# Scale, shift and the first input rows by quarters of the features, with rotary swaps as VectorE shuffles

## The reference, cut to what matters

```python
    cos, sin = _rope_tables(positions)
    c_act = jax.nn.silu(c)
    mod = (c_act @ w_ada[l] + b_ada[l])[:, None, :]
    shift1, scale1, gate1, shift2, scale2, gate2 = jnp.split(mod, N_MOD, axis=-1)
    h = _rmsnorm(x, g_mix[l]) * (1.0 + scale1) + shift1
    proj = h @ w_in[l]
    a_u, a_v, b_q, b_k, b_v, c_q, c_k, c_v = jnp.split(proj, splits, axis=-1)
    ...
    y_c = _dilated_window(_rope(c_q...), _rope(c_k...), c_v...)
    # _rope: x1, x2 = jnp.split(x, 2, axis=-1)   (halves of each head of 64)
    #        concatenate([x1 * cos - x2 * sin, x2 * cos + x1 * sin])
```

## Time and profile before

| | before |
|---|---|
| median of 3 runs | 935.67 us |
| profiled execution | 936.85 us |
| its span, first to last instruction | 935.0 us |
| PE busy | 907.0 us (97%) |
| DVE busy | 613.3 us (66%) |
| ACT busy | 497.1 us (53%) |

### The profile page before, as it was taken

The page is one execution under the profiler, slowest core; times in us unless marked ns, Lnnn a source line. Parts: engine busy times, 40 slices in busy tenths (PEclk is TensorE's granted clock), DMA queues, the critical chain, the costliest instruction groups (busy, mean ns, idle before and its releaser), DMA issues.

```text
span 935.0 us, 17321 instructions
## 1 busy us (share of the span) xinstructions
PE 907.0 (97%) x7189; PEld 839.9 (90%) x7189; DVE 613.3 (66%) x958; ACT 497.1 (53%) x729; POOL 0.2 (0%) x4
## 2 busy tenths in 40 slices
PE   5899999999999999999999999999999999999997
PEld 2688788899999999778999999998999999988886
DVE  0565685786776776787765555576886765566664
ACT  4537674754555567665644343346656653344333
POOL 0000000000000000000000000000000000000000
PEclk9899999999999999999999999999999999999999
DMA  9988757675556569415366565555442655555541
GB/s 351 369 292 275 271 182 249 211 254 204 171 175 218 180 169 179 105 46 163 109 216 195 195 195 196 179 181 180 128 143 95 222 176 172 188 186 181 181 135 45
DMA packets 130697, 176.78 MB, mean 189 GB/s; under 512 B 19696, under 2 KB 108188, under 8 KB 130620
## 3 DMA queue, kind: packets, MB, share of 16 engines
q1 hardware_dynamic: 129852, 173.51, 57.0%
q10 hardware_dynamic: 768, 2.16, 0.7%
HBM read 174.62 MB, written 1.05 MB: 188 GB/s over the span
## 4 chain that ended last, share of the span: by engine, by line
PE 84%; DVE 7%; ACT 4%; DMA 3%; issue 2%; SPq 0%; ACTq 0%; DVEq 0%
PE psum L1605 25%; PE psum L1597 21%; PE psum L1598 21%; PE psum L1601 4%; PE psum L1602 4%; DMA raw<-in_w_ada_dram 2%; DVE w_lo L956 2%; PE psum L1699 1%; ACT w_hi L526 1%; PE psum L2199 1%; PE psum L2154 1%; PE psum L2143 1%; PE psum L2133 1%; DMA raw<-in_w_in_dram 1%; DVE h_lo L994 1%
## 5 line engine op out<-in xcount | busy, mean ns | idle before, releaser
L526 ACT ACTIVATE w_hi<-raw 128x2048 fp32r<-128x2048 f32 (+1 forms) x139 | 264.5, 1905 | 147.4 <-PE psum L1605 122.1
L1597 PE MATMUL psum<-h_hi,w_hi 128*128 128x256 f32 x1352 | 328.7, 283 | 1.5 <-DVE h_lo L1128 1.1
L956 DVE TENSOR_TENSOR w_lo<-raw,w_hi 128x2048 fp32r<-128x2048 f32 (+1 forms) x139 | 313.2, 2278 | 22.2 <-ACT w_hi L526 22.1
L1598 PE MATMUL psum<-h_lo,w_hi 128*128 128x256 f32 x1352 | 324.5, 279 | 0.0
L1597 PEld LDWEIGHTS psum<-h_hi,w_hi 128*128 128x128 f32 x1352 | 254.4, 188 | 10.2 <-issue 7.2
L1598 PEld LDWEIGHTS psum<-h_lo,w_hi 128*128 128x128 f32 x1352 | 254.8, 188 | 0.8
L1605 PE MATMUL psum<-h_hi,w_lo 128*128 128x256 f32 x1352 | 186.9, 280 | 0.7 <-DVE w_lo L956 0.5
L1605 PEld LDWEIGHTS psum<-h_hi,w_lo 128*128 128x128 f32 x1352 | 170.3, 188 | 1.5 <-DVE w_lo L956 1.4
L1324 DVE SCALAR_TENSOR_TENSOR arena<-psum,rstd 128x256 f32<-128x256 f32 x64 | 26.9, 424 | 131.9 <-PE psum L1605 130.0
L1597 PE MATMUL psum<-a_hi,w_hi 128*128 128x256 f32 x464 | 110.6, 280 | 0.6 <-DVE a_lo L1311 0.4
L1598 PE MATMUL psum<-a_lo,w_hi 128*128 128x256 f32 x464 | 110.2, 279 | 0.0
(11 more groups left out here) (272 smaller groups left out, 899.3 us busy)
## 6 DMA issues: line engine op xcount, KB each, us to landing
raw<-in_mlp_w_in_dram SPq DMA_DIRECT2D x32, 1024.0 KB, 5.6
raw<-in_mlp_w_out_dram SPq DMA_DIRECT2D x32, 1024.0 KB, 7.1
raw<-in_w_ada_dram SPq DMA_DIRECT2D x24, 1024.0 KB, 7.6
raw<-in_w_up_dram SPq DMA_DIRECT2D x22, 1024.0 KB, 5.1
raw<-in_gla_w_in_dram SPq DMA_DIRECT2D x12, 1024.0 KB, 5.3
raw<-in_w_down_dram SPq DMA_DIRECT2D x11, 1024.0 KB, 5.4
raw<-in_w_in_dram SPq DMA_DIRECT2D x10, 1024.0 KB, 7.5
raw<-in_w_out_dram SPq DMA_DIRECT2D x4, 1024.0 KB, 5.9
```

The costliest lines, as they stand in the source:

```text
L526: act.activation(halved(w_hi, m % SPLIT_SLOTS, SPLITS[m]), halved(raw, r % RAW_SLOTS, SPLITS[m]), ACT.Copy).then_inc(*mark("w_hi", m))
L956: dve.tensor_tensor(halved(w_lo, m % SPLIT_SLOTS, key), halved(raw, r % RAW_SLOTS, key), halved(w_hi, m % SPLIT_SLOTS, key).bitcast(F32), ...
L1597: pe.matmul(dst, high, both[0], start=start, stop=False, skip_group_check=True)
L1598: return pe.matmul(dst, high, both[1], start=False, stop=False, skip_group_check=True)
```

## The change

- The condition chunks of scale and shift now hold 256 columns of all 1024 rows, so that one chunk gives a finished quarter of scale or of shift (`part`). `w_in` is loaded for the first four projection chunks (1024 output features) by 256 rows, that is by quarters of the input features (`rows_in`). The stream starts with four times scale quarter, shift quarter, input rows: 12 MB.
- Eight sums (four chunks of two tiles) are kept in banks 0 to 3 and grow from quarter to quarter (`rows_high`, `rows_low`); they are read in `evict`. The ring is banks 4 to 6 meanwhile.
- `turn_x` comes ahead of all condition chunks, and DVE copies half of x.
- Rotary: `w_hi` and `w_lo` of queries and keys are written with their columns in bands of 16, so that the swap is one within 32 lanes. DVE does it with a shuffle, five instructions of 128 x 512 or 128 x 256 for two tiles, and PE does nothing. The rounding of such rows is three instructions in place of one, on ACT and on DVE.
- Of the other condition chunks four come beside `in` 0 to 3 no more but beside the output projection.

```diff
-ADA_BESIDE = [0, 1, 1, 2, 1, 1, 1, 1, 2, 1, 1]
+ADA_BESIDE = {4: 1, 5: 1, 6: 1, 7: 1, 8: 1, 9: 1, 10: 2}
+ADA_BESIDE_OUT = [2, 1, 1, 0]
+FIRST_CHUNKS = 4
...
+    for q in range(4):
+        s += [("ada", 1, q), ("ada", 0, q), ("rows_in", q)]
...
+    s = [("setup",), ("turn_x",), ("root", 0), ("part", 1, 0), ("part", 0, 0), ("quarters", 0), ("rows", 1), ("mod", 1, 0),
+         ("mod", 0, 0), ("gains", 0, 0), ("total", 0), ("normed", 0, 0), ("round", 0), ("first", 0), ("round_low", 0)]
+    for q in range(1, 4):
+        s += [("rows_high", q - 1, 0), ("part", 1, q), ("rows_high", q - 1, 1), ("part", 0, q), ("mod", 1, q), ("gains", 0, q),
+              ("normed", 0, q), ("rows_low", q - 1, 0), ("mod", 0, q), ("rows_low", q - 1, 1), ("round", q), ("first", q),
+              ("sines",) if q == 2 else ("angles",) if q == 1 else ("round", 4), ("round_low", q)]
+    s += [("rows_high", 3, 0), ("rows_high", 3, 1), ("rows_low", 3, 0), ("rows_low", 3, 1),
+          ("evict", 0), ("rope", 0), ("evict", 1), ("round_low", 4), ("evict", 2), ("evict", 3)]
+    extra = {4: [("rope", 1), ("rope", 2), ("w_sp",)],
+             5: [("win_a", 0), ("win_a", 1), ("rows", 2), ("rows", 3), ("rows", 4), ("win_a", 2)],
...
+                    if SPLITS[m][0] == "rows_in":
+                        for h in range(2):
+                            act.activation(banded(w_hi, m % SPLIT_SLOTS)[:, :, :, h, :],
+                                           banded_raw(r % RAW_SLOTS)[:, :, :, h, :], ACT.Copy).then_inc(*mark("w_hi_banded", m, h))
+                        act.activation(w_hi[:, m % SPLIT_SLOTS, QK:CHUNK], raw[:, r % RAW_SLOTS, QK:CHUNK], ACT.Copy)\
+                            .then_inc(*mark("w_hi", m))
...
+            def part(p, q):
...
+                for j in range(2):
+                    for g in range(4):
+                        ins = pe.matmul(dst[32 * g:32 * g + 32, 0:S], c_rep[:, 4 * j + g, :], src[:, 4 * j + g, :], start=(j == 0),
+                                        stop=(j == 1), skip_group_check=True)
...
+            def rows_high(q, j):
...
+                for n in range(FIRST_CHUNKS):
...
+                    for m in range(2):
+                        high_by_both(first_sum(n, m), row_tile(w_hi, slot, j, n, m), (h_hi[:, k, :], h_lo[:, k, :]),
+                                     k == 0 and m == 0)
...
+                dve.wait_ge(*at("act_read", "in", n, 1))
...
+                dve.stream_shuffle(work[:, 2:4, :], both, SWAPPED).then_inc(*mark("rope_swapped", n))
+                dve.tensor_tensor(work[:, 0:2, :], both, angle_of(1), ALU.mult).then_inc(*mark("rope_cos", n))
...
+                dve.tensor_tensor(work[:, 2:4, :], work[:, 2:4, :], angle_of(0), ALU.mult).then_inc(*mark("rope_sin", n))
...
+                for m in range(2):
...
+                    dve.tensor_tensor(dst, work[:, m, :], work[:, 2 + m, :], ALU.add).then_inc(*mark("roped", n, m))
```

307 lines of the change are left out of this document (156 added, 151 removed).

## The result

The changed kernel takes 951.87 us (median of four runs, 950.28 to 956.91), against 935.71 us for the kernel before, run beside it (four runs, 935.48 to 935.76). The ratio is 1.0166, with a 95% interval of 1.0139 to 1.0193. It is slower, as forecast, but by twice the size: 16.2 us where 7.8 was forecast (943.5, with a range that ended at 948).

What follows compares the result with a forecast made beforehand. PE, busy 97%, was taken as the bound. Eight sums end at T = 60.2 (57.0 plus 3.2 for the clock); T - 52.33 gives +7.9 on 936.85, 944.7 profiled, median 943.5; eight in ten 937.5 to 948.

Steps and rivals of the forecast that it cites:

- PE's start: Start until the first product: PE starts products at 20.9, 11 us earlier than before, idle from 16.6 to 20.9.
- R3: Rival: rounding in bands of 16 columns costs twice for the banded three quarters, +6.6, 950 us; chance 8%.
- Gaps of about 1 us in each quarter: Chain behind each quarter's second part, 3.8 us beside 2.5 of PE work: 1.3 idle in three quarters, period 9.35.
- the late load ahead of the fourth: Scale chunk 3, started behind the angles, lands at 42.6, wanted at 41.5; with the rows behind it 2.5 us.
- R2: Rival: DVE's queue behind the sums does not hold PE, 9.6 us go, 933.8; 13% with anything else under 935.7.
- The clock. ... I take 3.2: Idle stretch ahead of first products: clock falls at 21.5, 6.8 us at half clock, 3.2 us lost, T = 60.2.
- 9.6 us of waits at full clock: Between the eight sums and in 6: PE waits 2.7 + 0.9 + 0.4 + 1.1 + 2.4 + 2.1; without them 16.0.
- R1: Rival: the clock does not fall, eight sums done at T = 57.0, +4.7, 940.3 us; chance 22%.
- 4.9 us from idle to the fall: Clock delay taken from the kernel before: falling 4.9 us after PE goes idle at 16.6, so at 21.5.
- The sentence on the free-running watch: Activity watch isn't reset by a kernel, so a same-length stretch can cost or not; leaves the fast case, T = 57.0.
- Behind in 6 I cost nothing: After in 6: four condition chunks beside the output projection have load room; the last wait, 0.7 us, may go or stay.
- 4.55 was forecast: Work done later, behind in 6: four condition chunks (3.96) and mod 2 (0.59), beside nothing, 4.55 us.

Runs made afterwards that it cites:

- e1_queue: Changed kernel with in 4's low part ahead of the first rotary turn on DVE, in 5 rounded right behind the sums' reads: 944.9 us, ratio 1.0072.
- e7_all: Changed kernel with DVE queue reordered, 34 identity transposes, later angles, chunks 2, 2, 0, 0, earlier rounding and small transposes, rows 2 to 4 before scores: 935.69 us, 0.9982.
- e13_warm: Changed kernel, nothing moved, with identity transposes filling every PE wait at whose end the clock was low: ratio 1.0105.
- e9_spread: e7_all with the four late condition chunks one to each part of the output projection (1, 1, 1, 1): ratio 1.0008.
- e10_back: e7_all with one more condition chunk beside each of in 4 to in 7, none beside the output projection: ratio 1.0045.
- e15_late: e7_all with the four late condition chunks one each beside in 8, in 9 and the output projection's first two parts: 934.8 us, ratio 0.9977.
- e5_angles: Changed kernel with the angles' work on DVE behind the low part of input rows 1 instead of ahead: ratio 1.0157.
- e6_out: Changed kernel with the four condition chunks beside the output projection issued 2, 2, 0, 0 in place of 2, 1, 1, 0: ratio 1.0140.
- e12_before_fill: Kernel before with 22 identity transposes in PE's longest idle stretch, ahead of its first products: ratio 1.0014.
- e8_before_fill: Kernel before with 34 identity transposes scheduled but none issued by PE, so the kernel before once more: ratio 0.9996.
- e3_fill: Changed kernel with 34 identity transposes on PE between the total of x and the first products: 948.72 us, ratio 1.0113.
- e16_nofill: e7_all without the 34 identity transposes: ratio 1.0008.

## Why the prediction was right, and why its size was wrong

**Right: PE's start.** 21.54 against 20.9, from the same chain, with the fall at 13 us in it; without it 20.0 to 20.3. The rounding that ACT does ahead of h took some 2.0, where the forecast has 2.2. ACT's two rows, then DVE's of the low part:

```profile
18.45 1.56 ACT L554 ACTIVATE w_hi<-raw 128x768 fp32r<-128x768 f32 x2
19.91 0.61 ACT L556 ACTIVATE w_hi<-raw 128x512 fp32r<-128x512 f32 x1
```

```profile
L993 DVE TENSOR_TENSOR w_lo<-raw,w_hi 128x768 fp32r<-128x768 f32 x8 | 7.3, 952 | 0.0
L995 DVE TENSOR_TENSOR w_lo<-raw,w_hi 128x512 fp32r<-128x512 f32 x4 | 2.7, 684 | 0.0
```

One banded instruction of 768 columns takes 0.84 us on ACT (the row merges two that overlap) and 0.95 on DVE. A straight line through the plain ones of 512 and of 2048 columns (0.62 and 1.90 on ACT, 0.68 and 2.28 on DVE) gives 0.83 and 0.95. R3 is out: its 950 lies nearest to the measured time of all the numbers in the forecast, and its cause isn't there. DVE's rows agree with the rule of the Trainium skill that the forecast set beside it (Vector Engine (DVE) Microarchitecture Reference, 5.2 Measured stream behaviour on trn2): runs of 16 adjacent words go at the full rate.

**Right: the places of the waits and their order.** Gaps of about 1 us in each quarter (1.3 forecast), the late load ahead of the fourth, in 4's low part (2.44; 2.7), in 5 (0.69 and 0.25; 0.9 and 0.4), the first scores (0.43; 1.1), rows (2.37; 2.4), third scores (2.00; 2.1): 8.2 us between the sums and in 6, where the forecast has 9.6. e1_queue, which changes only the order of steps on DVE and ACT there, takes that stretch from 27.5 to 20.4 us, so the order of the queues is the cause. R2 is out as the changed kernel stands, and e7_all shows what it would have taken.

**Wrong: "The clock. ... I take 3.2".** The forecast charges one fall, in the idle stretch ahead of the products, and then adds 9.6 us of waits at full clock. It had the waits and their lengths, but never asked of them what it asked of the first. e13_warm puts the four falls from 20 us to in 6 at 9.1 us in the profiled run: 5.9 more than the 3.2; the fall at 13 us adds 1.4 that the chain of the start made up elsewhere. The delay that the forecast took over, 4.9 us from idle to the fall, didn't hold either: PE goes idle at 17.6 and the clock falls at 19.7, 2.1 later. R1 was the opposite of what came: the clock did not stay, it fell six times in the first 220 us. The chance of that case (falls in several places) was nowhere in the list. The sentence on the free-running watch (the Trainium skill, TensorE: Matmul & The Clock Gate, What's actually happening) was used only to argue for fewer falls; the profiles show that nearly the same wait, ahead of the fourth quarter (2.87 and 2.79) or of in 4's low part (2.42 and 2.44), is followed by a fall in one kernel and not in the next, so it argues for more of them as well. That the waits of this kernel call the falls forth is shown by e13_warm; why one of them meets a fall and its like doesn't, no run shows.

**Wrong: "Behind in 6 I cost nothing".** The stretch from in 6 to the gate products grew by 8.8 us where 4.55 was forecast, and in every variant by at least 7. Condition work on PE is busy for 15.2 us where before has 10.2, and 4.0 more was foreseen. The last wait of the stretch, 0.83 before, is 2.31 for DMA and meets a fall; its chunk is loaded late:

```profile
160.82 2.29 SPq L531 DMA_DIRECT2D raw<-in_w_up_dram  x2
167.86 8.82 SPq L531 DMA_DIRECT2D raw<-in_w_ada_dram  x4
```

The last condition loads share the queue and the slots with up and out weights. In the kernel before, the loads in this stretch had room (share 0.70) because four chunks were behind them already. e9_spread, e10_back and e15_late show that of the places tried none takes the chunks in free: 10.4, 8.3 and 7.1 us more than before in this stretch. How the excess over 4.55 is split between waits, clock and work is not shown beyond the rows above.

**The ledger** of the profiled runs: 944.7 forecast; + 1.0 in the chain up to in 6; + 5.9 for falls up to in 6; + 4.2 from there to the gate products (8.8 less 4.55); + 1.1 behind them, where the last fall ends and profiles scatter by as much. That is 956.9. By the medians the miss is 8.4. The two runs of e13_warm with next to no fall, 944.5 and 945.2, split it roughly, an estimate from two runs that were made beside other runs of the kernel before: the forecast without a fall is 940.3 (R1), so 4 to 5 is not the clock, about what the stretch behind in 6 has too much; the falls take 7 in the median where 3.2 was charged, the other 4. It can't be had more closely, since what the falls cost differs between runs of one kernel: the changed kernel's four runs spread over 6.6 us. So do those of the kernel before beside the experiments, over 3.4 to 6.5 us; that its first four spread over 0.3 was luck.

## What to carry to other kernels

A wait on a busy TensorE can have two prices, its length and what the clock loses behind it, and the second belongs with a chance to each wait in the sum, not to the first alone. It is nothing where PE would have waited anyway, as at 412 us in the kernel before. Where a change moves loads later, compare the DMA share and the order on the queue at the new place with those at the old; a share that has room before the move is no proof that it has room after. When several waits stand in a row, mend them together: mending one (e5_angles) gained nothing that could be measured, mending most of them (e7_all) 16 to 17 us. And read the mean clock of every run beside its time: a kernel whose runs lie at 0.980 and 0.990 has no single profile that speaks for it.

## What the runs showed of the hardware that was not expected

The same wait met a fall of the clock in one kernel and none in the next. Ahead of the fourth quarter PE waits 2.87 us in the changed kernel and 2.79 in e1_queue: half clock from 54 to 60 in the first, full clock in the second. Ahead of in 4's low part it waits 2.42 in e5_angles, with a fall, and 2.44 in e6_out, without one. In e15_late the longest wait from 21 us on is 1.63, and the granted clock is 1.00 throughout its first 220 us. In e12_before_fill a stretch at 0.50 lasted from 26.3 to 36.5 with PE busy 8.28 of 9 us in it, longer than the 6.8 us of the kernel before.

A long wait isn't needed either. In the second block of the kernel before the clock falls at 412.4, where the last wait of PE is 0.87 us, and in the changed kernel at 432.7 behind 0.83. In e8_before_fill, the same program as before, and in most of the other profiles the same place is passed at 1.00.

34 identity transposes, 3.9 us of work that computes nothing, made one kernel 3 to 5 us faster (e3_fill) and another 2.4 (e7_all against e16_nofill). In the kernel before, 22 of them gained nothing.

A fall of the clock that PE spends ahead of a wait for ACT cost nothing: 3.72 us from L2154 to L2133 in the kernel before at half clock, 3.72 in the same program at full clock.
